# Two output halves by turns: the order of the fp32r products within a weight block

## The reference, cut to what matters

```python
# first block (d = 2048, FFN 5632)
u = h @ hgrn_w_in            # 2048 x 10240
m = gated_recurrences(u) @ hgrn_w_out
up = dwconv3(h @ ffn_w_in)   # 2048 x 11264
x = x + rmsnorm((silu(gate) * val) @ ffn_w_out)
# second block
proj = h @ w_in              # 2048 x 7184
x = x + mixed @ w_out
x = x + cross_attention(h, mem_n, w_xq, w_xkv, w_xo)
x = x + (silu(gate) * up) @ w_down      # up: h @ w_up, 2048 x 11264
return rmsnorm(x)
```

## Time and profile before

| | |
|---|---|
| median of three runs | 2681.29 us (2680.46 to 2681.52) |
| the profiled execution | 2680.03 us |
| its span, first to last instruction | 2678.2 us |
| TensorE, matmuls | 2667.0 us busy, 17616 instructions |
| VectorE | 1971.5 us busy |
| ScalarE | 1335.4 us busy |
| granted TensorE clock, mean | 0.999 of full speed |
| memory read | 477.63 MB, 179 GB/s over the span |

### The profile page before, as it was taken

The page is one execution under the profiler, slowest core; times in us unless marked ns, Lnnn a source line. Parts: engine busy times, 40 slices in busy tenths (PEclk is TensorE's granted clock), DMA queues, the critical chain, the costliest instruction groups (busy, mean ns, idle before and its releaser), DMA issues.

```text
span 2678.2 us, 47424 instructions
## 1 busy us (share of the span) xinstructions
PE 2667.0 (100%) x17616; PEld 2293.1 (86%) x17616; DVE 1971.5 (74%) x2721; ACT 1335.4 (50%) x1679; POOL 133.8 (5%) x138
## 2 busy tenths in 40 slices
PE   9999999999999999999999999999999999999998
PEld 8888888888888888888888888878888888888887
DVE  6888888878888888644466677767678888885444
ACT  6455555455444444433465556665554444444443
POOL 0221112210000000000000000000000000000000
PEclk9999999999999999999999999999999999999999
DMA  7555455564555555666645544455455555555554
GB/s 244 178 171 168 165 166 174 166 202 156 189 189 188 189 188 188 194 194 195 224 139 180 168 149 135 135 174 183 151 192 188 191 189 192 188 189 189 188 189 157
DMA packets 136197, 481.68 MB, mean 180 GB/s; under 512 B 14880, under 2 KB 19120, under 8 KB 135680
## 3 DMA queue, kind: packets, MB, share of 16 engines
q1 hardware_dynamic: 134160, 472.06, 53.7%
q0 software_dynamic: 1376, 7.46, 0.8%
q10 hardware_dynamic: 528, 0.26, 0.0%
HBM read 477.63 MB, written 2.10 MB: 179 GB/s over the span
## 4 chain that ended last, share of the span: by engine, by line
PE 93%; DVE 3%; issue 1%; DMA 1%; ACT 1%; DVEq 0%; ACTq 0%; SPq 0%
PE acc L443 37%; PE acc L445 19%; PE acc L466 8%; PE acc L468 8%; PE acc L467 8%; PE acc L415 4%; PE acc L416 2%; DVE wts L363 1%; DMA raw<-stream 1%; PE ps L1407 1%; ACT wts L356 1%; PE ps L741 1%; PE acc L928 1%; DVE cy L2314 1%; PE acc L561 0%
## 5 line engine op out<-in xcount | busy, mean ns | idle before, releaser
L443 PE MATMUL acc<-hs,wts 128*128 128x512 f32 x4640 | 1626.4, 394 | 0.0
L363 DVE TENSOR_TENSOR wts<-raw,wts 128x1024 fp32r<-128x1024 f32 x888 | 1062.0, 1227 | 511.7 <-ACT wts L356 511.0
L356 ACT ACTIVATE wts<-raw 128x1024 fp32r<-128x1024 f32 x888 | 913.3, 1054 | 831.9 <-PE acc L445 362.3
L445 PE MATMUL acc<-hs,wts 128*128 128x256 f32 x4640 | 1297.1, 280 | 0.0
L443 PEld LDWEIGHTS acc<-hs,wts 128*128 128x128 f32 x4640 | 871.1, 188 | 193.6 <-issue 0.8
L445 PEld LDWEIGHTS acc<-hs,wts 128*128 128x128 f32 x4640 | 871.5, 188 | 0.5
L466 PE MATMUL acc<-wts,acts 128*128 128x512 f32 x688 | 268.2, 390 | 0.5 <-DVE wts L363 0.5
L468 PE MATMUL acc<-wts,acts 128*128 128x512 f32 x688 | 267.7, 389 | 0.0
L467 PE MATMUL acc<-wts,acts 128*128 128x512 f32 x688 | 267.7, 389 | 0.0
L370 ACT ACTIVATE half<-acc 128x512 f32<-128x512 f32 x161 | 95.5, 593 | 158.0 <-PE acc L445 139.1
L466 PEld LDWEIGHTS acc<-wts,acts 128*128 128x128 f32 x688 | 129.2, 188 | 27.9 <-DVE wts L363 1.2
(11 more groups left out here) (361 smaller groups left out, 2172.6 us busy)
## 6 DMA issues: line engine op xcount, KB each, us to landing
raw<-stream SPq DMA_DIRECT2D x888, 512.0 KB, 4.1
xf<-xT SPq DMA_DIRECT2D x8, 256.0 KB, 6.4
raw<-stream SPq DMA_DIRECT2D x8, 256.0 KB, 6.6
fm<-memT POOLq DMA_DIRECT2D x2, 1024.0 KB, 7.3
fw<-stream POOLq DMA_DIRECT2D x2, 1024.0 KB, 11.6
memr<-memT POOLq DMA_DIRECT2D x1, 2048.0 KB, 9.8
outT<-memr SPq DMA_DIRECT2D x7, 256.0 KB, 2.9
KQ<-masks POOLq DMA_DIRECT2D x1, 448.0 KB, 5.7
```

The lines of the kernel that those rows point to most:

```text
L356: nc.scalar.activation(high, source, ACT.Copy).then_inc(hi_ready, 1)
L363: nc.vector.tensor_tensor(low, source, high.bitcast(F32), ALU.subtract).then_inc(lo_ready, 1)
L443: nc.tensor.matmul(acc[:, 2 * par + n, :], whi[:, b, c:c + P], src[:, kt, :], start=start, stop=False)
L445: mm = nc.tensor.matmul(acc[:, 2 * par + n, 0:T], wlo[:, b, c:c + P], src[:, kt, 0:T], start=False, stop=stop)
```

## The change

In multiply, the loop over q is now the outer one. For each row tile the two 512-column products are issued first, n = 0 and n = 1, and then the two 256-column ones, n = 0 and n = 1. Their operands, their destinations and their number are as before. The branch with tokens keeps its order and is written out ahead. The waits of n3 and n5 for the row tiles stand before each q. The side is advanced after q = 1 and q = 3, and `blk_used` is incremented by the last product (q = 3, n = 1).

```diff
-            for n in range(2):
-                for q in range(4):
-                    kt = 4 * kb + q
-                    start, stop = kt == 4 * first, kt == 4 * last + 3
-                    if norm in ("n3", "n5") and n == 0 and q:
-                        pe.wait_ge(NV[norm].sem, NV[norm].count(f"l{kb}{q}" if q < 3 else f"lo{kb}"))
-                    if tokens:
-                        mm = weigh_tokens(n, b, q, src, kt, par, start, stop)
-                        continue
-                    c = q * 256 + n * P
-                    nc.tensor.matmul(acc[:, 2 * par + n, :], whi[:, b, c:c + P], src[:, kt, :],
+            if tokens:
+                for c in range(2):
+                    for q in range(4):
+                        kt = 4 * kb + q
+                        mm = weigh_tokens(c, b, q, src, kt, par, kt == 4 * first, kt == 4 * last + 3)
+                    if c == 1:
+                        mm.then_inc(blk_used, 1)
+                    if side is not None:
+                        next(side, None)
+                return
+            for q in range(4):
+                kt = 4 * kb + q
+                start, stop = kt == 4 * first, kt == 4 * last + 3
+                if norm in ("n3", "n5") and q:
+                    pe.wait_ge(NV[norm].sem, NV[norm].count(f"l{kb}{q}" if q < 3 else f"lo{kb}"))
+                c = q * 256
+                for n in range(2):
+                    nc.tensor.matmul(acc[:, 2 * par + n, :], whi[:, b, c + n * P:c + (n + 1) * P], src[:, kt, :],
                                      start=start, stop=False)
-                    mm = nc.tensor.matmul(acc[:, 2 * par + n, 0:T], wlo[:, b, c:c + P],
+                for n in range(2):
+                    mm = nc.tensor.matmul(acc[:, 2 * par + n, 0:T], wlo[:, b, c + n * P:c + (n + 1) * P],
                                           src[:, kt, 0:T], start=False, stop=stop)
-                if n == 1:
+                if q == 3:
                     mm.then_inc(blk_used, 1)
-                if side is not None:
+                if side is not None and q % 2:
                     next(side, None)
```

## The result

The changed kernel takes 2699.84 us (median of four, 2699.71 to 2700.92) against 2680.88 us before: a ratio of 1.0072, 95% interval 1.0059 to 1.0085, so 19.0 us slower. The forecast was 2680.8 us with no change likeliest; the time lies 1.8 us above the upper end of the range, 2698.

A forecast was written before the change was run, and what follows sets the result against it. TensorE, busy throughout, was taken as the bound. 2336 quads x 0 and -0.5 us in the openings gave -0.5 us, so the 2681.29 us median became 2680.8 us; range 2675 to 2698 us.

The forecast's parts named there:

- What bounds the kernel: Whole kernel: TensorE is busy throughout, so time is the number of products times their start-to-start pitch.
- The banks at 0: Reordered products in multiply: changing the accumulation bank at every product was put at 0 gain.
- the bank counts: Rival, all reordered products: the surcharge is the price of staying in a bank; 109 us less, 2572 us; chance 0.06.
- two short products in a row: New 256-after-256 step in each quad: taken as 120 ns, bounds 7 us less to 159 us more; quad 694 ns, change 0.
- fixed surcharge of 13 ns on every product: TensorE products, long or short: each costs 13 ns beyond its columns, giving 227 and 120 ns.
- That rival: Reordered pairs a few ns slower, as with stationary activations: 3.75 ns a quad to a pair, 8.8 to 17.5 us; chance 0.14.
- The starved load: Rival, 256 after 256: weight loads in a row take over 120 ns; at 188 ns, +159 us, 2840; chance 0.04.
- The short step is shorter: Rival, step after a 256-column product: 117 ns whatever follows, no loss elsewhere; -7 us, 2674; chance 0.08.
- The openings: First groups with norm n3 or n5: 12 waits of about 43 ns for low parts become hidden, 0.5 us less.
- The rival of a big gain: Reordered products: staying in a bank causes the surcharge, so changing banks saves 109 us, to 2572 us; chance 0.06.
- less what the feed of weights gives back: Reservation on the 109 us gain from changing banks: the feed of weights would return some of it, size not given.

The follow-up runs named there:

- e1: Changed kernel, order kept, but all 16 products of a weight block go to one bank: 2813 ns a block, 2699.5 us in all.
- e2: Kernel before, order kept, but every product changes banks in blocks 1 to 3: 2773 ns in all blocks, 2680.14 us beside 2680.66.
- e4: Against the kernel before, per row tile 512 and 256 columns into bank 0, then 512 and 256 into bank 1: 2773 ns a block, 2681.04 us.
- e16: Long and short by turns, banks changing every second product, timed with eleven executions against the kernel before: 2681.41 us against 2680.86, ratio 1.0002.
- e9: Changed kernel's weights, banks and rows, but long and short products by turns: 2773 ns in blocks 1 to 3, 2900 in block 0; 2696.63 us in all.
- e10: Kernel before's weights, banks and rows, but lengths in twos (even row tiles 512 columns, odd 256): 2813 ns a block.
- e8: Kernel before with its short product cut from 256 to 128 columns: 340 ns a pair, 2664.88 us against 2679.69.
- e7: Changed kernel with 512-column products cut to 256 in blocks 1 to 3: short steps 117 ns each; loops 2789 ns a block in up1, 2781 in up2.

## Why the prediction was wrong

*What bounds the kernel* held for this change: the time moved with the products' pitch. It gave no size to the feed of weights, which stands close behind in the loops and would have eaten most of a gain there. *The banks at 0* held too: the bank changes read in the earlier trace rows told the truth, and e1, e2, e4 and e16 say so with the sequence of lengths held fixed. The advice of the Trainium skill ("Perfetto Trace Analysis", "Matmul Optimizations") to use all banks for instruction-level parallelism was rightly given no weight here, as far as turns between two banks test it: e2 changes banks at every product of blocks 1 to 3, and its blocks are as long as before to the nanosecond. No run turned through all eight. Rival "the bank counts" is out. The Trainium skill ("TensorE: Matmul & The Clock Gate", "Back-to-back issue gap") gives N/2.4 + 2.5 ns for an isolated matmul at 2.4 GHz. No order of these fp32r products comes down to it: the least mean surcharge of one length in a row is 10 to 12 ns, with short products; the plain fp32 ones do.

*The step that failed is the sum that closes "two short products in a row",* 227 + 227 + 120 + 120 = 694 ns a quad. The unseen step it worried about, 256 to 256, was right (118 against 120; never the 188 of the upper bound). The term taken as known was wrong: the step behind a 512-column product was put at 227, a cost of the wide stage, and with moving activations it is 233 before another long product and 235 before a short one. The quad is 233 + 235 + 118 + 117.5, or 703. Even in the old order that step was 229 to 230 and the short one 117 to 118, as the 0.23 and 117 of the earlier trace rows say; the split into 227 and 120 had the right sum there and the wrong parts. Under it lies the claim of a **fixed surcharge of 13 ns on every product**: two patterns were fitted by two numbers, and that left nothing to test it with. The short product pays 117 to 119 - 107 = 10 to 12 ns in every order; the long one pays 229 - 213 = 16 by turns and 20 to 22 otherwise, and in the wide stage 13. Only the mean of the two by turns is 13. The third pattern in the old trace did test it, and failed it: with stationary activations pairs took 2.80 us for eight, not 2.77. That its 350 ns is nearly the 352 of the change may be chance: the roles are others there, and no run ties the two together. The prediction read that row, and kept it as a rival with 0.14.

*That rival* had the right sign, the right place and too small a price: 3.75 ns a quad to a pair, where the change costs 5 ns a pair (10 a quad, 23.4 us). Its top, 17.5 us, set the range's upper end at 2698. The reason for keeping the chance low was "the operands here are those of the first pattern"; e9 and e10 show that with the same roles the order of the operands doesn't enter and the sequence of lengths does.

*The starved load* is out for 256 columns: short steps of 117 ns stand in a row. It is a limit for the product of 128 columns (e8). *The short step is shorter* was right about the short step (117 to 119) and wrong that nothing else is lost.

*The openings:* the term of -0.5 us was sound. In the changed kernel the blocks concerned grew by 0.5 us less than their neighbours (0.2 in up1, 0.3 in the mix input). In pairs by turns, where blocks keep their length, the first four blocks of up1 take 0.14 us less and those of the mix input 0.28, but a block three further on in up1 takes 0.14 us more, so that up1 keeps nothing of it.

*The rival of a big gain* would not have paid in full even if banks had counted: with pairs of 340 ns the loop of up2 still ran at 346, by the feed of weights. The prediction's words "less what the feed of weights gives back" named this without a size.

## What to carry to other kernels

Where TensorE is never idle, the order of products of two lengths has a price of its own: measure long after long, short after short and the two by turns in the very stage that is to change, and take no step's cost from a stage where the operands play other roles: here the two roles even differ in which sequence is the cheaper for the long product. A cost law that is fitted with as many patterns as it has numbers is a guess; look in the trace for a third pattern, and believe the one that misses. Turning between accumulation banks from product to product gave nothing here, with or without the order. And before a change that may gain, ask what stands just behind the bound: here the weights came at about the pace at which TensorE used them.

## What the runs showed of the hardware

- With moving activations in fp32r at 2.4 GHz, 512-column products in a row take 234 ns, 256-column ones 117 to 119, the two by turns 347 a pair, in twos 352, in fours 352.5, in eights 351 to 352; the short step is the same in all, and the cause of the 5 ns on the long one is open.
- Cutting the short product from 256 to 128 columns saves 7 ns of a pair's 347, where the columns alone are worth 53: two weight loads of 128 columns never start less than 108 ns apart in these loops.
- In the kernel with short products alone in three blocks of four (e7) TensorE waits for weights, up to 2.7 us at a time, and the granted clock is 0.92 in the mean of a stretch, so for a part of it the engine ran at 1.2 and not 2.4 GHz; it was 1.00 in every stretch shown above. Waits first, then the stretch (TensorE, loads, VectorE, ScalarE, GpSimd, and then the clock):

```profile
PE acc L462 <- DVE wts L363: 155.9, 90, 2.7
...
640.00:860.00 220.00, 185.59 (x1255) 172.67 (x1254) 181.91 (x269) 95.72 (x109) 0.00 (x0) 0.92 0.56 187
```
